# Layer norms whose centre is first taken from the first tiles, in a four-layer hybrid transformer

## The chip, the cores and the metric

One core of a Trainium2 chip runs the whole program. The metric is the device time of one execution in microseconds. PE is TensorE (PEld its weight loads), DVE VectorE, ACT ScalarE, POOL GpSimd, SP SyncE, which issues most DMAs.

## What is computed

```
for i in range(DEPTH):                       # 4 layers: attention, gated delta net, gated linear attention, attention
    mod = (s_lat @ ada_w[i] + ada_b[i]).reshape(bsz, 6, 1, d)      # d = 1024, and modc likewise from s_ctx
    u = modulate(x, mod[:, 0], mod[:, 1])                          # t * (1 + scale) + shift
    y, yc = mixer(u, uc, ...)
    x = layer_norm(DN_ALPHA * x + mod[:, 2] * y, ln_g[i, 0], ln_b[i, 0])
    h = modulate(x, mod[:, 3], mod[:, 4])
    x = layer_norm(DN_ALPHA * x + mod[:, 5] * conv_glu(h, ...), ln_g[i, 1], ln_b[i, 1])
    # the same for the 256 context tokens, in all layers but the last
def layer_norm(t, g, b):
    mu = jnp.mean(tf, -1, keepdims=True)
    var = jnp.mean(jnp.square(tf - mu), -1, keepdims=True)
    return ((tf - mu) * lax.rsqrt(var + NORM_EPS)).astype(t.dtype) * g + b
```

All in float32. There are 256 context tokens and 256 others, 512 columns in all; in the last layer only 256 are carried past the keys and values.

## The kernel before

The residual stream x lies transposed: eight tiles of 128 features, each 128 partitions by 512 tokens. A layer norm's sums therefore run over partitions and tiles, and PE makes them. Every float32 product of weights and activations is three products in fp32r: both operands are split into a rounded high part and a low rest (w_hi, w_lo by POOL, lines 586 and 589; u_hi by ACT, line 697; u_lo by DVE, line 1765). Weights come in units of 1 MB, in two buffers, and are split in four pieces each. The order on each engine is written out by hand, an engine's instructions run in that order, and semaphores count between engines.

A norm (w = 0 after the mixer, w = 1 after the feed-forward part) goes like this. `residual` (DVE, line 1770) adds a finished tile from PSUM to x, two instructions. `mean_sum` (PE, line 1538) sums a tile of x over its features into strips of 32 partitions, four float32 matmuls that show as eight instructions. In w = 0 the last two tiles are made by `tile_unit` (line 1102), one after the other, with mean sums between them; in w = 1 the last down unit finishes tile after tile (line 1704). When all eight tiles are summed, ACT copies the strips to `srow` (line 942), `rows_of` (PE, line 1544) spreads them over 128 partitions, `norm` on DVE subtracts the mean from eight tiles (line 2278), ACT squares each (`norm_stats`, line 950), PE sums the squares (`variance_sums`), ACT takes the root (line 953), DVE the reciprocal (line 2282), PE spreads it, and DVE multiplies (line 2287). Then `make_u` on ACT scales and shifts each tile (line 693) and rounds it, DVE takes the rest with `u_low`, PE starts the next unit's products (`column_unit`, line 1090) tile after tile, and POOL writes the new x (`new_x`, line 598), released by the same u_hi.

While a norm after a mixer runs, PE also makes four of the next layer's conditioning products (`ada_block_unit`, line 1513), whose weights ACT requests. DVE shifts the condition columns for them (`condition_moved`). At the start of the program layer 0's first conditioning products (`ada_unit`, 1504) read eight blocks of 1 MB; their sums are copied (`ada_copy`), turned into columns (`ada_turn`) and made into scale and shift (`modulation`); the first `make_u` follows.

In attention, PE transposes two blocks of probabilities into banks 4 and 5 (line 1171), ACT copies both at once (line 731).

```
def variance_sums(l, w):
    for t in range(KT):
        eng.wait_ge(sq_ready, pe.next(sq_ready))
        mm = strips(l, bank[STAT[w][1]], meanw[:, 0:32], sq[:, t % 4, :], t == 0, t == KT - 1)
        mm.then_inc(var_ready if t == KT - 1 else sq_used, 1)
    eng.wait_ge(dev_ready, pe.next(dev_ready))
    rows_of(l, bank[STAT[w][3]]).then_inc(rstd_ready, 1)
```

## Time and profile before

| | |
|---|---|
| median of 3 runs | 2803.31 us (2802.9, 2803.31, 2812.05) |
| the profiled execution | 2810.65 us, of which the span is 2808.9 |
| PE busy | 2617.1 us (93%) |
| POOL, DVE, ACT busy | 1559.1, 1166.7, 828.2 us |
| granted TensorE clock, mean | 0.966 of full |

A row of a timeline gives start, length, engine, line, operation, what is written and read with shapes, the count of instructions in it, and in brackets the idle time before it and what ended that. A row that merges several instructions gives the time from the first one's start to the last one's end.

### The profile page before, as it was taken

To read this page: it belongs to the slowest core of one execution; us is meant where nothing else is said; L and a number is where in the kernel's file an instruction comes from. 1 tells how busy PE (TensorE), PEld (TensorE's weight loads), DVE (VectorE), ACT (ScalarE), POOL (GpSimd) and SP (SyncE) were. 2 spreads that over 40 slices of the span, in tenths; PEclk is the share of its full clock that TensorE was granted. 3 is DMA by queue.
4 is the path that set the end of the run, shared out by engine and by line. 5 is a ranking of instruction groups with operands and counts; after the bars stand their busy time and mean duration, and the time that the engine had idled before them with its cause. 6 is when DMAs were issued, how large, how long until landed. Compare 5 with 4: busy or idle time off the path is not lost. (4 is left out here: it accounts for less than half of the span.)

```text
span 2808.9 us, 45504 instructions
## 1 busy us (share of the span) xinstructions
PE 2617.1 (93%) x16413; PEld 2105.6 (75%) x16413; DVE 1166.7 (42%) x2177; ACT 828.2 (29%) x1556; POOL 1559.1 (56%) x1601
## 2 busy tenths in 40 slices
PE   6999999999899799999999989898999999787998
PEld 4766677787687699767778768896677787677997
DVE  2364322222469677432222320584322222463555
ACT  2253322211540444142210132351312211353542
POOL 2402666666558222466667656785666665715664
PEclk8999999999999899999999989999999999898998
DMA  6343455423123000255542222002455422201553
GB/s 243 115 132 123 156 172 167 155 91 102 50 76 90 31 2 2 90 165 179 177 132 95 75 63 90 31 1 75 152 178 179 150 90 90 75 31 61 180 177 108
DMA packets 217162, 305.61 MB, mean 109 GB/s; under 512 B 7331, under 2 KB 155550, under 8 KB 217023
## 3 DMA queue, kind: packets, MB, share of 16 engines
q1 hardware_dynamic: 179007, 228.16, 24.6%
q10 hardware_dynamic: 38016, 75.50, 8.3%
q8 instruction: 98, 1.61, 0.2%
q14 instruction: 41, 0.34, 0.0%
HBM read 302.60 MB, written 1.05 MB: 108 GB/s over the span
## 5 line engine op out<-in xcount | busy, mean ns | idle before, releaser
L589 POOL TENSOR_TENSOR w_lo<-w_raw,w_hi 128x512 fp32r<-128x512 f32 x688 | 900.6, 1309 | 102.3 <-POOL w_hi L586 82.2
L586 POOL TENSOR_SCALAR w_hi<-w_raw 128x512 fp32r<-128x512 f32 x688 | 450.7, 655 | 880.5 <-PE bank L1090 597.0
L1090 PE MATMUL bank<-u_lo,w_hi 128*128 128x512 f32 (+1 forms) x2144 | 810.8, 378 | 31.2 <-DVE u_lo L1765 20.2
L1090 PE MATMUL bank<-u_hi,w_lo 128*128 128x512 f32 (+1 forms) x2144 | 793.6, 370 | 0.0
L1090 PE MATMUL bank<-u_hi,w_hi 128*128 128x512 f32 (+1 forms) x2144 | 793.3, 370 | 0.0
L1090 PEld LDWEIGHTS bank<-u_lo,w_hi 128*128 128x128 f32 x2144 | 410.5, 191 | 167.3 <-issue 89.7
L1090 PEld LDWEIGHTS bank<-u_hi,w_hi 128*128 128x128 f32 x2144 | 410.4, 191 | 68.9
L1090 PEld LDWEIGHTS bank<-u_hi,w_lo 128*128 128x128 f32 x2144 | 411.4, 192 | 63.2
L1673 PE MATMUL bank<-gs_lo,w_hi 128*128 128x512 f32 (+1 forms) x576 | 211.4, 367 | 2.2 <-POOL w_lo L589 2.2
L1673 PE MATMUL bank<-gs_hi,w_lo 128*128 128x512 f32 (+1 forms) x576 | 210.8, 366 | 0.0
L1673 PE MATMUL bank<-gs_hi,w_hi 128*128 128x512 f32 (+1 forms) x576 | 210.8, 366 | 0.0
L2360 DVE SCALAR_TENSOR_TENSOR cv<-bank,vec,cv 128x510 f32<-128x510 f32 (+1 forms) x88 | 59.5, 676 | 344.4 <-ACT cv L1010 344.4
L2385 DVE TENSOR_TENSOR gs_lo<-g,gs_hi 128x512 fp32r<-128x512 f32 (+1 forms) x88 | 102.1, 1171 | 239.7 <-ACT gs_hi L1047 239.5
L1010 ACT ACT_TABLE_LOAD x27 | 34.6, 1283 | 431.2 <-PE bank L1090 431.2
L2377 DVE TENSOR_TENSOR g<-cv,bank 128x512 f32 (+3 forms) x88 | 50.8, 617 | 229.1 <-PE bank L1090 218.8
L1047 ACT ACTIVATE gs_hi<-g 128x512 fp32r (+3 forms) x88 | 49.4, 574 | 314.6 <-PE bank L1673 256.2
L1770 DVE SCALAR_TENSOR_TENSOR x<-bank,gat,x 128x256 f32<-128x256 f32 x112 | 48.7, 479 | 192.2 <-PE bank L1090 95.1
L1673 PEld LDWEIGHTS bank<-gs_lo,w_hi 128*128 128x128 f32 x576 | 108.2, 188 | 23.2 <-issue 3.6
L1673 PEld LDWEIGHTS bank<-gs_hi,w_lo 128*128 128x128 f32 x576 | 108.4, 188 | 19.5
L1673 PEld LDWEIGHTS bank<-gs_hi,w_hi 128*128 128x128 f32 x576 | 108.2, 188 | 19.5
L598 POOL TENSOR_SCALAR x<-x,vec 128x512 f32<-128x512 f32 (+1 forms) x56 | 67.5, 1204 | 64.7 <-ACT u_hi L697 64.7
L618 POOL TENSOR_TENSOR bAT<-bD,con 128x512 f32<-128x512 f32 x16 | 20.3, 1273 | 129.5 <-ACT bD L832 129.5
(334 smaller groups left out, 3835.8 us busy)
## 6 DMA issues: line engine op xcount, KB each, us to landing
w_raw<-in_ffn_w_up SPq DMA_DIRECT2D x88, 1024.0 KB, 7.2
ada_w<-in_ada_w ACTq DMA_DIRECT2D x72, 1024.0 KB, 5.2
w_raw<-in_ffn_w_down SPq DMA_DIRECT2D x44, 1024.0 KB, 4.9
ada_w<-in_ada_w SPq DMA_DIRECT2D x16, 1024.0 KB, 5.1
w_raw<-in_gdn_w_in SPq DMA_DIRECT2D x16, 1024.0 KB, 5.7
w_raw<-in_attn_w_qkv SPq DMA_DIRECT2D x12, 1024.0 KB, 5.0
w_raw<-in_gla_w_in SPq DMA_DIRECT2D x12, 1024.0 KB, 5.3
ada<-in_ada_w SPq DMA_DIRECT2D x8, 1024.0 KB, 13.4
```

Source lines behind the costliest of these rows:

```text
L586: eng.tensor_scalar(w_hi[:, q, :], src, 1.0, 0.0, ALU.mult, ALU.add).then_inc(pool.own, pool.step())
L589: eng.tensor_tensor(w_lo[:, q, :], src, w_hi[:, q, :].bitcast(F32), ALU.subtract).then_inc(w_split, 1)
L598: eng.tensor_scalar(x[:, t, T], x[:, t, T], vec[:, LNG(l, w, t):LNG(l, w, t) + 1], vec[:, LNB(l, w, t):LNB(l, w, t) + 1], ALU.mult, ALU.ad ...
L618: eng.tensor_tensor(AT[:], Dm[:], wide(tri[d]), ALU.mult).then_inc(pat_ready, 1)
L1010: eng.activation(cv[:, m, T], bank[m][:, T], ACT.Identity, bias=vec[:, bass.ds(f + CONVB(l), 1)], scale=vec[:, bass.ds(f + CONVW(l, 1), 1) ...
L1047: eng.activation(gs_hi[:, slot, T], gf, ACT.Copy).then_inc(gs_h, 1)
L1090: mm = eng.matmul(bank[banks[m]][:, T], w[:, q, c:c + P], v[:, k, T], start=(k == 0 and n == 0), stop=(k == KT - 1 and n == 2))
L1673: mm = eng.matmul(bank[b][:, T], w[:, q, j * P:(j + 1) * P], v[:, s, T], start=(start and q < 2 and n == 0), stop=(stop and q >= 2 and n = ...
L1770: ins = eng.scalar_tensor_tensor(x[:, t, half(s)], bank[b][:, half(s)], gat[:, l, w, t, s:s + 1], x[:, t, half(s)], ALU.mult, ALU.add)
L2360: eng.scalar_tensor_tensor(v3(cv[:, m, :], 1, 256), v3(bank[m][:], 0, 255), w0, v3(cv[:, m, :], 1, 256), ALU.mult, ALU.add).then_inc(dve.o ...
L2377: eng.tensor_tensor(g[:, bass.ds(i * 2 + m, 1), T].rearrange("p a n -> p (a n)"), cv[:, m, T], bank[2 + m][:, T], ALU.mult).then_inc(g_don ...
L2385: eng.tensor_tensor(gs_lo[:, slot, T], gf, gs_hi[:, slot, T].bitcast(F32), ALU.subtract).then_inc(gs_ready, 1)
```

## The change: a provisional centre, a split start, single copies

Norms. From the first tiles (four of eight in w = 0, two in w = 1; `CENTRE`) a provisional mean is taken and spread over the partitions by one fp32r product per 128 tokens while the last tiles are being multiplied. It is subtracted from each tile as it is finished (`centred`), or ahead of its residual for the last tiles (those from `RAW` on). Squares of the centred tiles are summed in the order `SQUARES`, most of them between the last tiles' products. At the end the true mean's distance d from the centre comes from the same strips; the variance is the mean square less d squared, and each tile is corrected by a second subtraction (`move`), two tiles ahead of the product with the inverse deviation. The conditioning products move: one between the two spreadings, one behind them, two into the first unit of the up projection, behind its tiles 0 and 1.

Start. The conditioning blocks are read in the order 0, 2, 1, 3; after the first four (of eight halves) tiles 0 to 3 are modulated, and the other halves are multiplied ahead of tile 0 and tile 3 of the first projection. The first projection's weights are read in between, the masks behind everything.

Attention. Each transposed block is copied by itself.

```
@@ variables and loads
-STAT = ((4, 5, 6, 4), (0, 1, 2, 7))
+STAT = ((4, 5, 6, 4, 2), (0, 1, 2, 7, 3))
+CENTRE = (4, 2)
+RAW = (6, 4)
+SQUARES = ((0, 1, 6, 2, 3, 4, 5, 7), (4, 0, 5, 1, 6, 2, 7, 3))
             for n in range(ADA_FIRST):
+                if n == ADA_FIRST // 2:
+                    load(column(a["attn_w_qkv"][0], 0))
...
@@ ACT, norm_stats
-                eng.wait_ge(ms_ready, act.next(ms_ready))
-                eng.activation(srow[strips, :], bank[STAT[w][0]][strips, 0:P], ACT.Copy).then_inc(mc_ready, 1)
+                eng.wait_ge(cs_ready, act.next(cs_ready))
+                eng.activation(drow[strips, :], bank[STAT[w][0]][strips, 0:P], ACT.Copy)
+                eng.activation(crow[strips, :], bank[STAT[w][0]][strips, 0:P], ACT.Copy, scale=KT / CENTRE[w]).then_inc(cc_ready, 1)
...
@@ ACT, attention
-                        eng.wait_ge(pt_ready, act.next(pt_ready))
-                        eng.activation(apt[:, j % 3, :, 0:NK], banks[:, 4:6, 0:NK], ACT.Copy).then_inc(pts_ready, 1)
+                        for m in range(2):
+                            eng.wait_ge(pt_ready, act.next(pt_ready))
+                            eng.activation(apt[:, j % 3, m, 0:NK], bank[4 + m][:, 0:NK], ACT.Copy).then_inc(pts_ready, 1)
@@ PE, w = 0
+                    if m == 0 and inside:
+                        eng.wait_ge(cc_ready, pe.next(cc_ready))
+                        centre_rows(l, 0)
+                    elif m == 0:
                         for t in (4, 5):
                             mean_sum(l, 0, t)
+                    elif inside:
+                        mean_sum(l, 0, 6)
+                        for i in range(4):
+                            square_sum(l, 0, i)
                     else:
...
+                        for i in range(4, 7):
+                            square_sum(l, 0, i)
+                        mean_sum(l, 0, 7)
@@ PE, w = 1, behind down tile t
+                    if t == 3:
+                        eng.wait_ge(cc_ready, pe.next(cc_ready))
+                    if t >= 1:
+                        mean_sum(l, 1, t - 1)
+                    if t == 3:
+                        centre_rows(l, 1)
+                    for i in {5: (0,), 6: (1, 2), 7: (3, 4)}.get(t, ()):
+                        square_sum(l, 1, i)
@@ DVE, norm
+                eng.wait_ge(ms_ready, dve.next(ms_ready))
+                eng.tensor_tensor(drow[strips, :], drow[strips, :], bank[STAT[w][0]][strips, 0:P], ALU.add).then_inc(dl_ready, 1)
...
+                eng.tensor_tensor(d2row[strips, :], drow[strips, :], drow[strips, :], ALU.mult).then_inc(dve.own, dve.step())
...
+                    eng.tensor_tensor(srow[strips, :], bank[STAT[w][1]][strips, 0:P], d2row[strips, :], ALU.subtract).then_inc(vr_ready, 1)
...
                 for t in range(KT + 1):
                     if t < KT:
+                        eng.wait_ge(dve.own, moved[t])
                         ins = eng.tensor_tensor(x[:, t, S], x[:, t, S], rstd, ALU.mult)
...
+                        if t + 2 < KT:
+                            move(t + 2)
+                    if t == 1 and behind:
+                        behind()
                     if t >= 1 and not final:
                         u_low(l, t - 1)
@@ PE, start, behind each u tile's wait of the first projection
+            def first_tile(k):
+                if k == 0:
+                    ada_half_block(2)
+                if k == 1:
+                    ada_turn(ADA_ORDER[2])
+                if k == 3:
+                    ada_half_block(3)
+                    ada_turn(ADA_ORDER[3])
+                u_tile(k)
```

What stands on PE behind the last tile of w = 0 in layer 0, before (a row of 32x128 is a strip sum, of x for the mean or of sq for the variance; L1544 spreads rows, L1513 is a conditioning product):

```order
L1513 MATMUL bank<-ada_w,sT 32x512 [waits tile_finished,ada_loaded_0]
L1513 MATMUL bank<-ada_w,sT 32x512 x3
L1538 MATMUL bank<-x,con 32x128 [waits residual_ready]
L1538 MATMUL bank<-x,con 32x128 x3
L1538 MATMUL bank<-x,con 32x128 [waits residual_ready]
L1538 MATMUL bank<-x,con 32x128 x3
L1544 MATMUL bank<-srow,con 128x128 [waits mean_strips_copied]
L1544 MATMUL bank<-srow,con 128x128 x3
L1513 MATMUL bank<-ada_w,sT 32x512 [waits ada_loaded_1]
L1513 MATMUL bank<-ada_w,sT 32x512 x3
L1538 MATMUL bank<-sq,con 32x128 [waits square_ready]
L1538 MATMUL bank<-sq,con 32x128 x3
```

After the change, the same place from the last mean sum on (L1575 strip sums, L1581 spreads rows, L1545 conditioning), three more square sums standing ahead of it:

```order
L1575 MATMUL bank<-x,con 32x128 [waits residual_ready]
L1575 MATMUL bank<-x,con 32x128 x3
L1575 MATMUL bank<-sq,con 32x128 [waits square_ready]
L1575 MATMUL bank<-sq,con 32x128 x3
L1581 MATMUL bank<-drow,con 128x128 [waits mean_from_centre_ready]
L1581 MATMUL bank<-drow,con 128x128 x3
L1545 MATMUL bank<-ada_w,sT 32x512 [waits ada_loaded_0]
L1545 MATMUL bank<-ada_w,sT 32x512 x3
L1581 MATMUL bank<-srow,con 128x128 [waits inverse_deviation_ready]
L1581 MATMUL bank<-srow,con 128x128 x3
L1545 MATMUL bank<-ada_w,sT 32x512 [waits ada_loaded_1]
L1545 MATMUL bank<-ada_w,sT 32x512 x3
```

The mean sum of tile 6 and four square sums have left this place; they now stand in the middle of the last tile's products:

```order
L1575 MATMUL bank<-x,con 32x128 [waits residual_ready]
L1575 MATMUL bank<-x,con 32x128 x3
L1575 MATMUL bank<-sq,con 32x128 [waits square_ready]
L1575 MATMUL bank<-sq,con 32x128 x3
L1575 MATMUL bank<-sq,con 32x128 [waits square_ready]
L1575 MATMUL bank<-sq,con 32x128 x3
L1575 MATMUL bank<-sq,con 32x128 [waits square_ready]
L1575 MATMUL bank<-sq,con 32x128 x3
L1575 MATMUL bank<-sq,con 32x128 [waits square_ready]
L1575 MATMUL bank<-sq,con 32x128 x3
L1132 MATMUL bank<-u_lo,w_hi 128x512
L1132 MATMUL bank<-u_hi,w_lo 128x512
```

On DVE, from the last residual to the first u_lo, before (L1770 residual, L2278 subtraction, L2282 reciprocal, L2287 product with the inverse deviation, L1765 u_lo):

```order
L1770 SCALAR_TENSOR_TENSOR x<-bank,gat,x 128x256 [waits tile_finished]
L1770 SCALAR_TENSOR_TENSOR x<-bank,gat,x 128x256
L2278 TENSOR_TENSOR x<-x,bank 128x512 [waits mean_ready]
L2278 TENSOR_TENSOR x<-x,bank 128x512 x7
L1779 COPY sT_kept<-sT 128x240 [waits ada_multiplied]
L1782 MEMSET sT 128x8x2 [waits dve_step]
L1783 COPY sT<-sT_kept 128x8x30
L2282 RECIPROCAL srow<-srow 128x128 [waits deviation_ready]
L2287 TENSOR_TENSOR x<-x,bank 128x512 [waits inverse_deviation_rows_ready]
L2287 TENSOR_TENSOR x<-x,bank 128x512
L1765 TENSOR_TENSOR u_lo<-u_66,u_hi 128x512 [waits u_hi_ready]
```

After the change (L1868 residual, L2391 and L2393 the distance and its square, L2406 the variance, L2399 correction, L2425 product):

```order
L1868 SCALAR_TENSOR_TENSOR x<-bank,gat,x 128x256 [waits dve_step,tile_finished]
L1868 SCALAR_TENSOR_TENSOR x<-bank,gat,x 128x256
L2391 TENSOR_TENSOR drow<-drow,bank 128x128 [waits mean_strips_ready]
L2393 TENSOR_TENSOR d2row<-drow 128x128 [waits mean_from_centre_ready]
L2406 TENSOR_TENSOR srow<-bank,d2row 128x128 [waits variance_ready,dve_step]
L2411 RECIPROCAL srow<-srow 128x128 [waits deviation_ready]
L2399 TENSOR_TENSOR x<-x,bank 128x512 [waits mean_ready]
L2399 TENSOR_TENSOR x<-x,bank 128x512
L2425 TENSOR_TENSOR x<-x,bank 128x512 [waits dve_step,inverse_deviation_rows_ready]
L2399 TENSOR_TENSOR x<-x,bank 128x512
L2425 TENSOR_TENSOR x<-x,bank 128x512 [waits dve_step]
L2399 TENSOR_TENSOR x<-x,bank 128x512
```

The eight subtractions have left the place behind the last residual, and each product is now followed by a correction two tiles ahead; the first u_lo follows three rows of condition columns later.

## Rows read from the trace of the kernel before

**Rows 1.** Busy time by stretch of the span, core 0, the columns as its head says
```profile
core 0: us, PE busy (x) PEld busy (x) DVE busy (x) ACT busy (x) POOL busy (x), PEclk, DMA share, GB/s
0.00:48.50 48.50, 22.63 (x136) 13.64 (x136) 12.21 (x26) 4.28 (x8) 5.14 (x10) 0.88 0.87 309
299.60:315.90 16.30, 12.66 (x129) 5.50 (x129) 9.33 (x18) 8.10 (x15) 8.30 (x9) 0.81 0.59 195
709.30:725.50 16.20, 8.38 (x104) 4.61 (x104) 8.78 (x15) 8.01 (x15) 8.19 (x9) 0.71 0.00 0
2576.40:2587.40 11.00, 5.85 (x50) 3.81 (x49) 5.54 (x14) 5.08 (x14) 7.99 (x9) 0.80 0.17 49
```

**Rows 2.** Timeline of layer 0's first norm: start us, length, engine, line, operation
```profile
286.95 0.64 PE L1538 MATMUL bank<-x,con 128*32 128x128 f32 x16
...
299.62 0.87 DVE L1770 SCALAR_TENSOR_TENSOR x<-bank,gat,x 128x256 f32<-128x256 f32 x2 [5.41 <-PE bank L1102]
...
302.82 4.87 DVE L2278 TENSOR_TENSOR x<-x,bank 128x512 f32<-128x512 f32 x8 [2.32 <-PE bank L1544]
...
308.90 0.37 ACT L953 ACTIVATE srow<-bank,con 128x128 f32<-128x128 f32 x1 [0.55 <-PE bank L1538]
309.30 0.95 DVE L2282 RECIPROCAL srow<-srow 128x128 f32<-128x128 f32 x1 [1.09 <-ACT srow L953]
...
310.30 2.08 PE L1544 MATMUL bank<-srow,con 128*128 128x128 f32 x8 [1.48 <-DVE srow L2282]
...
312.31 3.64 PE L1513 MATMUL bank<-ada_w,sT 128*32 128x512 f32 x16
312.42 1.28 DVE L2287 TENSOR_TENSOR x<-x,bank 128x512 f32<-128x512 f32 x2 [2.17 <-PE bank L1544]
...
313.22 1.09 ACT L693 ACTIVATE u<-x,aff 128x256 f32<-128x256 f32 x2 [3.96 <-DVE x L2287]
...
314.35 0.63 ACT L697 ACTIVATE u_hi<-u 128x512 fp32r<-128x512 f32 x1
...
315.01 0.69 DVE L1765 TENSOR_TENSOR u_lo<-u,u_hi 128x512 fp32r<-128x512 f32 x1 [1.31 <-ACT u_hi L697]
315.08 1.26 POOL L598 TENSOR_SCALAR x<-x,vec 128x512 f32<-128x512 f32 x1 [7.43 <-ACT u_hi L697]
```

**Rows 3.** Timeline of layer 0's second norm, same columns
```profile
698.21 0.88 DVE L1770 SCALAR_TENSOR_TENSOR x<-bank,gat,x 128x256 f32<-128x256 f32 x2 [0.45 <-PE bank L1704]
...
707.28 0.43 PE L1538 MATMUL bank<-x,con 128*32 128x128 f32 x8
...
709.34 0.88 DVE L1770 SCALAR_TENSOR_TENSOR x<-bank,gat,x 128x256 f32<-128x256 f32 x2 [1.07 <-PE bank L1704]
...
710.76 0.28 ACT L942 ACTIVATE srow<-bank 128x128 f32<-128x128 f32 x1 [24.42 <-PE bank L1538]
...
711.09 1.16 PE L1544 MATMUL bank<-srow,con 128*128 128x128 f32 x8 [0.40 <-ACT srow L942]
...
722.11 1.28 DVE L2287 TENSOR_TENSOR x<-x,bank 128x512 f32<-128x512 f32 x2 [2.17 <-PE bank L1544]
```

**Rows 4.** Timeline of the last layer's first norm
```profile
2585.19 0.75 DVE L2287 TENSOR_TENSOR x<-x,bank 128x256 f32<-128x256 f32 x2 [0.80 <-PE bank L1544]
```

**Rows 5.** DMA rate in 40 slices of the first 70 us, and a timeline row
```profile
GB/s 0 271 285 7 357 358 233 407 405 407 398 387 382 392 386 383 392 386 383 392 385 383 353 349 347 125 1 0 0 0 195 380 25 0 0 0 0 74 368 162
...
48.49 0.77 PE L1090 MATMUL bank<-u_lo,w_hi 128*128 128x512 f32 x1 [3.61 <-DVE u_lo L1765]
```

**Rows 6.** Timeline of POOL and DVE in the first make_u, and u_lo's min/median/max ns
```profile
45.96 1.26 POOL L589 TENSOR_TENSOR w_lo<-w_raw,w_hi 128x512 fp32r<-128x512 f32 x1
...
47.19 0.62 POOL L586 TENSOR_SCALAR w_hi<-w_raw 128x512 fp32r<-128x512 f32 x1
...
47.45 0.90 DVE L1765 TENSOR_TENSOR u_lo<-u,u_hi 128x512 fp32r<-128x512 f32 x1 [2.05 <-ACT u_hi L697]
...
L1765 DVE TENSOR_TENSOR u_lo<-u,u_hi x64: 424/692/1820, 47.5 to 2593.5; 128x512 fp32r<-128x512 f32 x56, 128x256 fp32r<-128x256 f32 x8
```

**Rows 7.** ACT's waits from 131 to 262 us (total, times, longest), and a timeline row
```profile
ACT apt L731 <- PE bank L1171: 38.3, 32, 2.9
...
2485.42 1.02 ACT L731 ACTIVATE apt<-bank 128x1024 f32<-128x1024 f32 x1 [0.72 <-PE bank L1171]
```

More of the change, by code:

```diff
@@ L2270, in upper, with centred @@
                 dve.skip(w_done, 4)
-            def norm(l, w, final=False, behind_mean=None):
+            def centred(l, w, t, ahead=False):
                 S = toks(l)
-                mean = bank[STAT[w][2]][:, S]
-                strips = slice(S.start // P * 32, P)
-                eng.wait_ge(mean_ready, dve.next(mean_ready))
-                for t in range(KT):
-                    eng.tensor_tensor(x[:, t, S], x[:, t, S], mean, ALU.subtract).then_inc(c_ready, 1)
-                if behind_mean:
-                    behind_mean()
-                eng.wait_ge(std_ready, dve.next(std_ready))
-                eng.reciprocal(srow[strips, :], srow[strips, :]).then_inc(dev_ready, 1)
-                rstd = bank[STAT[w][3]][:, S]
+                ins = eng.tensor_tensor(x[:, t, S], x[:, t, S], bank[STAT[w][2]][:, S], ALU.subtract)
+                if ahead:
+                    ins.then_inc(dve.own, dve.step())
+                else:
+                    ins.then_inc(c_ready, 1)
@@ L2334, in _ @@
                         dve.skip(w_done, 4)
+                        centre_seen(l, 0)
+                        for t in (6, 7):
+                            centred(l, 0, t, ahead=True)
+                        ahead = dve.count()
+                        for t in (0, 1):
+                            centred(l, 0, t)
                     for m in range(2):
@@ L2337, in _ @@
                             eng.wait_ge(tile_done, dve.next(tile_done))
+                            eng.wait_ge(dve.own, ahead)
                         residual(l, 0, 2 * n + m, (n % 2) * 2 + m)
+                        if (n, m) == (3, 0):
+                            for t in range(2, RAW[0]):
+                                if t >= CENTRE[0]:
+                                    eng.wait_ge(raw_read, dve.next(raw_read))
+                                centred(l, 0, t)
                 more = l + 1 < LAYERS
-                norm(l, 0, behind_mean=condition_moved if more else None)
+                norm(l, 0, behind=condition_moved if more else None)
                 per = {conv_c: 2, silu_done: 2, w_done: 8, own["dve"]: 2}
```

242 lines of the change are left out of this document (168 added, 74 removed).

## The prediction

> **What bounds the kernel now.** TensorE is busy nearly all the time, so a change can only pay where it waits. I read first the table of stretches, from a sublayer's last tile to the next one's first product, and the start [rows 1]. The reader is to see that such a stretch lasts 16.3, 16.2 and (last layer, half the tokens) 11.0 us, that PE's work in it is small products in half to three quarters of the time, and that the granted clock averages 0.71 to 0.81. There are eight of them, three of each of the first two kinds and two of the third: 3 x 16.3 + 3 x 16.2 + 2 x 11.0, some 120 of 2809 us. The start passes 48.5 us before the first projection.
>
> The timeline of one norm after the mixer [rows 2] gives the chain. Let T be the start of the last residual (299.62). The mean's rows are there at T+3.2, where eight subtractions start; squares follow at their pace until the root at T+9.3; reciprocal, rows at half clock (2.08 us), and the first product with the inverse deviation starts at T+12.8; call that moment R. From R on ACT sets the pace: 1.09 + 0.63 us a tile, measured 1.66 with the overlap; PE starts at R+3.5. The norm after the feed-forward part has the same chain, T = 709.34, R = T+12.8 [rows 3].
>
> **The norm after the mixer, three layers of 512 tokens.** Into PE's busy time come two detours from the tile products. What a detour costs: residuals come 0.88 + 0.45 us apart without a mean sum between the tiles and 0.88 + 1.07 with one [rows 3], some 0.6 more (I count 0.58; a tile is six products there, one each 0.22 to 0.23). Sixteen of its small instructions show as 0.64, eight as 0.43 [rows 2, 3], so a sum costs 0.2 and leaving the tile products 0.38. The four centre products cost at most a sum's 0.2: 0.6 us with the detour. Mean of tile 6 and four square sums: 0.38 + 5 x 0.2 = 1.4. T moves by +2.0. DVE gets eight provisional subtractions (0.61 us from start to start, 4.87 for eight [rows 2]) between the residuals; a tile is 24 products, 5.5 us on PE, so they fit.
>
> Behind T, with row durations: residual 0.88, strips at 1.42 [rows 3], a 128x128 addition I take as 0.2 (bounds: nothing and the 0.37 of ACT's root [rows 2]) gives 1.65. Beside it the square, a pass of ACT like u_hi's 0.63, and its sum 0.43 with 0.2 of latency give the variance at 2.15, the subtraction 2.4, root 0.37, reciprocal 0.95: 3.8. On PE the mean's rows (1.16 at full clock [rows 3]) end at 3.1, the conditioning product that stands between at 4.15 (1.8 at half clock, two in 3.64 [rows 2]; 1.07 at full), the deviation's rows at 5.4. DVE corrects tiles 0 and 1 meanwhile. R = old T + 2.0 + 5.4 = T+7.4 where T+12.8 was: **5.4 us** earlier.
>
> Not all of it lasts. Each of six tiles now has a correcting subtraction between its product and its u_lo: 0.61 + 0.61 + 0.69 = 1.9 us on DVE against ACT's 1.66. Counted through (moving the condition columns too, 0.65 us ahead of the first u_lo), the last u_lo comes at R+15.9, before it was R+14.8: 1.1 back. The two conditioning products that filled the wait now stand behind tiles 0 and 1 of the up projection, 1.07 each at full clock and 1.8 at half; PE's slack per tile is 1.9 - 1.37, so that most hides; I take 0.5 back, between 0 and 2.7 (6.8 us at half clock would cost 3.4 on PE, of which 0.7 lies under POOL's rounding of the next piece). Net 3.8 a norm, **11.4 us** for three. Their second weights are requested behind tile 0's u_hi, beside the next up weights: 0 to 2 us late, in the same bound.
>
> **The norm after the feed-forward part, three layers.** One more detour (0.58), the centre rows 0.2, three square sums 0.6, and 0.1 where the square of tile 5 comes late: T+1.45. DVE now does subtraction, residual, subtraction per tile, 2.2 us, against PE's 2.0 to 2.3: even. After T: two raw tiles are still to be centred (to 2.15), three squares in ACT's order end at 3.4, their sums, then mean rows at 3.1 to 4.3, the last square's sum 4.65, difference, root, correction of tile 0, reciprocal at 6.4, rows at 7.7, or 8.6 at half clock. Half clock is nearer: this stretch has 0.71 [rows 1], and the rows of this step took 2.08 in rows 2. R saves 12.8 - 1.45 - 8.65 = 2.7; the slower loop returns 0.4 (no moving of columns). Net 2.3, **6.9 us** for three.
>
> **The last layer** has 256 tokens: R-T is 8.7, from the stretch's start to 2585.19 [rows 1, 4]. By halved durations (0.34 from one product to the next: two end 0.75 after the start, one lasts 0.41) the first norm gets 1.3 + 4.1, gain 3.3, loop back 0.5: **2.8**. The final norm gains 2.2 and does six subtractions more in its last loop, 6 x 0.34: **0.2**.
>
> **Squared mean on DVE.** It reads SBUF twice while POOL rounds pieces. In the start such an operation, u_lo, took 0.90 where 0.69 is usual, and ended 0.54 after POOL's instruction [rows 6]. The new one can wait nothing or a piece's w_lo, 1.26; most of its wait is covered by the square's sum; 0.2 x 7: **-1.4 us**. The Trainium skill, page "SBUF — State Buffer", section "Who interferes with whom", says that a VectorE instruction with two SBUF inputs and a GpSimd instruction that reads SBUF exclude each other for a whole instruction; by that rule the term's upper end is right.
>
> **The start.** Before, all eight conditioning blocks are read first: the first product is at 48.49 [rows 5]. DMA moves 380 to 390 GB/s there, 2.7 us for a block of 1 MB [rows 5]. Now masks move behind, and four blocks suffice for tiles 0 to 3. I get the fourth block at 27, modulation at 31 to 32, u_lo(0) at 35; but PE then reads blocks five and six before tile 0 (landed at 35), and seven and eight before tile 3. At half clock (6 x 0.43 a tile, twice the above, 1.8 a pair of blocks) tile 3 is reached at 50 and tile 7 ends near 61, at full clock near 55. Before it ended near 62 (eight tiles from 48.49 by ACT's 1.66). Gain 1 to 7; **3 us**, nearer to half clock, since PE is mostly idle there. The mask's cast (1.16) stands before the last u_lo, its cost is in the 61.
>
> **Attention.** ACT's copy of both transposes (1.02 [rows 7]) becomes two, 0.6 each by u_hi's 0.63; the first starts half a transpose set earlier and the last ends 0.4 earlier, if ACT is free; it waited 38.3 us for transposes in 32 pairs [rows 7]. Between 16 x 0.2 lost (layer 3, if ACT binds) and 0.4 in half of 48 pairs won: -3 to +9, I take **2 us**, below the middle, as PE is the bound of most pairs.
>
> **Sum**: 11.4 + 6.9 + 2.8 + 0.2 - 1.4 + 3 + 2 = 24.9. The profiled execution took 2810.65, so it would take 2786. It stands 7.3 above the median of the runs, 2803.31; against that I forecast **2778 us**. 0.5% is 14 us, about what a measurement of this kernel can tell.
>
> **Rivals.**
> A, the clock stays up. Today rows of 1.2 us take 2.1, the conditioning products 1.8. If the shorter wait keeps full clock, 0.9 more for each rows step and 0.8 to 1 in the first unit: about 2 us x 7, gain 39, **2763 us**. For it: the gap shrinks by a third. Against: today it falls although sums run in between.
> B, the first up or projection unit gives it back. With half clock over its first 7 us PE needs 2.57 a tile against 1.9 supplied, and late conditioning weights add up to 2. Then 1.5 a mixer norm, 0.5 a feed-forward norm, 1.5 in the last layer, 1 at the start: gain 8.5, **2795 us**. For it: the end of the unit, not its start, passes the gain on. Against: six columns' u_lo already came slower than PE's 1.37.
> C, slower: u_lo is locked out by POOL. Until now u_lo and POOL's new x (L598) are released by the same u_hi, and DVE goes 70 ns ahead: 0.69 for u_lo, 1.26 for POOL [rows 2]. Now DVE is in a product or correction at that moment and POOL starts first. If u_lo then loses 0.9 (the longest seen, 1.82 [rows 6], loses 1.13), 56 times, it is 50 us: **2828 us**. The whole gain is gone from 25 / 56 = 0.45 us each. Against: POOL's 1.26 includes its wait behind u_lo, 0.6, so alone it should last some 0.7 and be over when DVE comes to u_lo, about 0.7 after u_hi. If 1.26 were POOL's true length, u_lo would wait 0.5 more a tile: 28 us, **2806**. That a lock lasts for the whole instruction is what the page named above says of it.
> That the change does not do what it says can be at the start: tiles 0 to 3 wait for the later blocks anyway. That is in B.
>
> **Chances.** Forecast (2768 to 2788) 0.50; A 0.15; B 0.26; C 0.09. Faster: the forecast, A and the best edge of B, 0.67. Same: the rest of B, 0.24. Slower: C, 0.09. The forecast's own range is 2768 to 2788; down to 2755 takes in A with attention's upper bound, up to 2805 takes in B with a start of nothing and attention lost.
>
> **What would show it.** In a mixer norm, R at T+5 to 6 from the last residual, the tile 7 later by 2; in a feed-forward norm T+8 to 9. DVE's period 1.9 in the first unit and its u_lo at 0.69; if it is over 1.1, C. The table of stretches should show some 11 and 13 us instead of 16.3, and the unit behind 0.5 to 1 more. First product of a projection near 36, but the second unit of projections only about 3 us earlier. Wrong would be: square sums that wait in the tile products for over 0.5 us, a first unit longer by over 3 us, or a start that gains nothing.

## The result and the profile after

The changed kernel takes 2774.60 us (median of 6 runs, 2771.59 to 2777.97), the kernel before 2803.11 (6 runs, 2799.18 to 2812.05): ratio 0.9899, 95% interval 0.9882 to 0.9917, 28.5 us less. The forecast was 2778. The profiled execution took 2774.4, its span is 2772.6; before they were 2810.65 and 2808.9, so the two traces lie 36.3 us apart, 8 more than the medians.

The stretches of [rows 1], in the changed kernel, same columns (busy time by stretch):

```profile
core 0: us, PE busy (x) PEld busy (x) DVE busy (x) ACT busy (x) POOL busy (x), PEclk, DMA share, GB/s
0.00:37.10 37.10, 16.23 (x103) 9.24 (x103) 10.43 (x24) 8.06 (x13) 7.11 (x12) 0.94 0.90 321
295.20:305.00 9.80, 5.95 (x74) 3.26 (x73) 8.51 (x17) 4.37 (x8) 8.41 (x10) 1.00 0.45 134
699.00:710.20 11.20, 4.69 (x74) 3.14 (x73) 8.65 (x16) 4.79 (x10) 8.22 (x9) 0.91 0.00 0
2541.00:2548.20 7.20, 2.77 (x29) 2.04 (x29) 5.60 (x13) 2.45 (x6) 6.55 (x8) 0.99 0.00 0
```

The stretches of 16.3, 16.2 and 11.0 us have become 9.8, 11.2 and 7.2 us, and the granted clock stays at 1.00, 0.91 and 0.99 where it was 0.81, 0.71 and 0.80. So far the stretches did better than forecast. As in the prediction, T is the start of a norm's last residual and R the start of its first product with the inverse deviation. The chain in layer 0's first norm, which answers to [rows 2] (timeline; T is 295.24):

```profile
295.24 0.88 DVE L1868 SCALAR_TENSOR_TENSOR x<-bank,gat,x 128x256 f32<-128x256 f32 x2 [4.48 <-PE bank L1132]
...
296.99 0.59 DVE L2393 TENSOR_TENSOR d2row<-drow 128x128 f32<-128x128 f32 x1
...
297.19 1.16 PE L1581 MATMUL bank<-drow,con 128*128 128x128 f32 x8
...
297.94 0.40 ACT L978 ACTIVATE srow<-srow,con 128x128 f32<-128x128 f32 x1 [1.16 <-DVE srow L2406]
...
298.38 0.95 DVE L2411 RECIPROCAL srow<-srow 128x128 f32<-128x128 f32 x1 [0.47 <-ACT srow L978]
...
299.38 1.16 PE L1581 MATMUL bank<-srow,con 128*128 128x128 f32 x8
...
300.58 0.69 DVE L2425 TENSOR_TENSOR x<-x,bank 128x512 f32<-128x512 f32 x1
```

R is at T+5.34, forecast T+5.4; the deviation's rows take 1.16 us, not 2.08. What comes behind R is where the forecast was too kind:

```profile
302.98 0.47 DVE L1877 COPY sT_kept<-sT 128x240 f32<-128x240 f32 x1
...
303.50 0.72 DVE L1881 COPY sT<-sT_kept 128x240 f32<-128x240 f32 x1
...
304.14 0.67 DVE L1863 TENSOR_TENSOR u_lo<-u,u_hi 128x512 fp32r<-128x512 f32 x1
...
304.96 0.47 PE L1118 MATMUL bank<-u_lo,w_hi 128*128 128x512 f32 x1 [3.42 <-DVE u_lo L1863]
...
307.38 1.77 PE L1545 MATMUL bank<-ada_w,sT 128*32 128x512 f32 x8
307.73 0.93 DVE L1863 TENSOR_TENSOR u_lo<-u,u_hi 128x512 fp32r<-128x512 f32 x1
...
310.66 1.06 PE L1545 MATMUL bank<-ada_w,sT 128*32 128x512 f32 x8
```

The first product now starts at R+4.38 (before R+3.47), since the condition columns are moved ahead of the first u_lo. The conditioning products take 1.77 us at half clock and 1.06 at full; PE works without a gap up to the second unit at 321.08. The half clock has not gone. It has moved out of the stretch into the first unit's opening: from 305.0 to 309.0 the granted clock is 0.57. In the kernel before it was 0.50 from 312.0 to 316.0, ahead of the unit, and 0.91 in the unit's first 4 us.

By norm, from both traces (before to after; "tile stage" is from the first product of the last 48 ahead of T up to T, "unit" from R to the first product of the second unit):

```
                     tile stage      R-T                      unit                        in all
mixer, layers 0-2    12.1 to 14.0    12.8/13.0/13.0 to 5.34   17.8/17.9/17.8 to 20.5/21.5/20.4   -2.8/-2.1/-3.0
feed-fwd, 0-2        14.1 to 16.0    12.8 to 7.7/8.6/8.5      23.9/27.4/17.6 to 25.0/28.5/18.6   -2.1/-1.2/-1.5
mixer, layer 3       10.2 to 11.7     8.7 to 4.9              11.4 to 12.6                       -1.2
final                 8.5 to 10.1     8.6 to 6.0              12.6 to 14.3 (to the end)          +0.6
```

That is 13.3 us in all for the eight norms, where 19.9 were forecast (11.4 + 6.9 + 2.8 + 0.2 - 1.4). What made the total right anyway was in no step of the forecast. Busy time of the down projection's 432 products in the kernel before (layer 0, then layer 3), then in the one after:

```profile
594.30:695.00 100.70, 100.69 (x432) 81.12 (x432) 1.00 0.28 94
2726.70:2777.60 50.90, 50.13 (x432) 49.64 (x432) 1.00 0.49 166
```
```profile
585.00:682.90 97.90, 97.88 (x432) 81.00 (x432) 1.00 0.29 97
2688.70:2741.10 52.40, 52.03 (x432) 51.86 (x432) 1.00 0.48 160
```

The same 432 products at the same full clock take 2.8 us less in each of layers 0 to 2 (8.5 us in all) and 1.5 more in layer 3. The change has no hunk in that loop. But its new buffer one_r takes 64 bytes ahead of g, gs_hi and gs_lo (g is the gated activation that the down projection reads, gs_hi and gs_lo are its two halves). By the program's sizes, counted from its first buffer, w_hi, w_lo, u_hi and u_lo lie at multiples of 128 bytes in both kernels; gs_hi and gs_lo lay 64 past one before and lie on one now.

### The profile page after: what moved, and what is told of

Same layout as the page of the kernel before. It is cut to its first block and busy times, and to the rows that moved or that the text cites. A ratio compares the mean times of both kernels' runs of the same rounds, so it can differ in the third digit from the quotient of the medians.

```text
span 2772.6 us, 45769 instructions
## 1 busy us (share of the span) xinstructions
PE 2592.8 (94%) x16441; PEld 2100.9 (76%) x16441; DVE 1211.5 (44%) x2278; ACT 838.6 (30%) x1614; POOL 1544.2 (56%) x1601
## 3 DMA queue, kind: packets, MB, share of 16 engines
HBM read 302.60 MB, written 1.05 MB: 110 GB/s over the span
## 5 line engine op out<-in xcount | busy, mean ns | idle before, releaser
L1118 PE MATMUL bank<-u_lo,w_hi 128*128 128x512 f32 (+1 forms) x2144 | 811.1, 378 | 39.2 <-DVE u_lo L1863 26.9
L2539 DVE TENSOR_TENSOR g<-cv,bank 128x512 f32 (+3 forms) x88 | 50.8, 618 | 228.2 <-PE bank L1118 217.9
L1868 DVE SCALAR_TENSOR_TENSOR x<-bank,gat,x 128x256 f32<-128x256 f32 x112 | 48.7, 480 | 161.1 <-PE bank L1118 93.4
L1038 ACT ACTIVATE cv<-bank,vec 128x512 f32<-128x512 f32 (+1 forms) x88 | 58.8, 718 | 105.8 <-PE bank L1118 105.5
## 6 DMA issues: line engine op xcount, KB each, us to landing
ada<-in_ada_w SPq DMA_DIRECT2D x8, 1024.0 KB, 13.6
```

The costliest lines, as they stand in the source:

```text
L1038: eng.activation(cv[:, m, T], bank[m][:, T], ACT.Identity, bias=vec[:, bass.ds(f + CONVB(l), 1)], scale=vec[:, bass.ds(f + CONVW(l, 1), 1) ...
L1118: mm = eng.matmul(bank[banks[m]][:, T], w[:, q, c:c + P], v[:, k, T], start=(k == 0 and n == 0), stop=(k == KT - 1 and n == 2))
L1868: ins = eng.scalar_tensor_tensor(x[:, t, half(s)], bank[b][:, half(s)], gat[:, l, w, t, s:s + 1], x[:, t, half(s)], ALU.mult, ALU.add)
L2539: eng.tensor_tensor(g[:, bass.ds(i * 2 + m, 1), T].rearrange("p a n -> p (a n)"), cv[:, m, T], bank[2 + m][:, T], ALU.mult).then_inc(g_don ...
```

## The experiments

Each was timed together with the kernel before on the same chip; its ratio to that is what is compared.

**1. The 64 bytes alone.**

```diff
         warm = sb("warm", [P, 1])
+        pad = sb("pad", [P, 16])
```

> The kernel before with 64 unused bytes behind the buffer `warm`, so that every buffer of the layer stages (the gated g, its halves gs_hi and gs_lo, q, k, v) lies 64 bytes higher, as the new buffer one_r puts it in the changed kernel; not an instruction differs. Theory 'layout': the place of gs_hi and gs_lo sets the rate of the down projection; its 432 products then take 97.8 us instead of 100.7 in each of layers 0 to 2 and 52.4 instead of 50.9 in layer 3, and the kernel is some 7 us faster (2796). Rival 'instructions': the down projection gained through the changed work between its products; then the loop stays at 100.7 and the time at 2803.

Measured 0.9973 (0.9961 to 0.9984), 7.6 us faster. The loop in this run, layers 0 and 3:

```profile
593.90:691.80 97.90, 97.90 (x432) 81.00 (x432) 1.00 0.29 97
2713.10:2766.00 52.90, 52.23 (x431) 51.90 (x432) 1.00 0.48 159
```

**2. The change without them.** The buffer is laid into unused bytes.

```diff
-        one_r = sb("one_r", [P, TT], F32R)
+        one_r = sb("one_r", [P, TT], F32R, at=top[0] - 32)
```

> The changed kernel with one_r laid into the unused bytes behind `warm`, so that the buffers of the layer stages lie where they lay before the change; not an instruction differs. Theory 'layout': the down projection goes back to 100.7 us (layer 3 to 50.9) and the kernel takes 7 us more than the changed one, 2782. Rival 'instructions': loop 97.8, time 2775.

Measured 0.9939 (0.9924 to 0.9954), median 2786.88: 11 us slower than the change by the ratios. The loop in layers 0 and 3:

```profile
586.90:687.60 100.70, 100.69 (x432) 81.12 (x432) 1.00 0.28 94
2705.40:2756.80 51.40, 50.23 (x432) 49.90 (x432) 1.00 0.48 164
```

Theory "layout" holds in both directions, and some 7 to 11 of the 28.5 us are a side effect. The loops themselves account for 7 of them (three times 2.8, less 1 to 2 in layer 3).

**3 and 4. Attention alone, start alone.** The edits are the diff's hunks of these two parts on the kernel before.

> The kernel before with only the copy of the transposed probabilities split in two. By the prediction's term: 2 us faster (between 3 slower and 9 faster), 2801; the attention stages themselves then show it. Rival: ACT has no time to spare in these pairs, and the second instruction per pair costs 0.2 each, 48 of them, so 2806 or more, or in layer 3 alone 3 us. Down projection as before, 100.7.

Measured 0.9984 (0.9973 to 0.9995): 4.5 us faster, 1.4 to 7.5. This run's own trace can't place it: from the second projection unit to T, layer 3's mixer takes 155.3 us, and the four traces with unchanged attention and unchanged norms have it anywhere from 155.4 to 158.2. Beside the changed norms it shows: up to the tile stage the same stretch takes 144.9 us with the old copy (experiment 5, one trace) and 140.5 to 142.1 in the eight traces with the new one. So layer 3 gained some 3 us there, and the prediction's loss in layer 3, if ACT binds, did not come.

> The kernel before with only the changed start (four conditioning blocks ahead of tiles 0 to 3, masks later, the rest between the tiles of the first unit). By the prediction: 3 us faster (1 to 7); the changed kernel's trace has the end of the first unit at 57.5 instead of 62.5, so 5 us and 2798 if all of that reaches the end; first product at 37, end of the first unit 57.5. Rival: the masks and weights that now come later, or the conditioning work in the unit, cost it again within the attention of layer 0, then 2801 to 2803.

Measured 0.9993 (0.9980 to 1.0005): 2 us faster, between 1.4 slower and 5.6 faster, so the gain is not clear of noise. Its trace has the first unit's end at 58.1 instead of 62.5. Other runs with the same start suggest why the median says less. The changed kernel, then the run of experiment 6, both from 37 us on (busy time by stretch):

```profile
37.00:49.00 12.00, 9.74 (x56) 6.73 (x53) 3.85 (x9) 2.95 (x6) 2.97 (x3) 0.91 0.98 344
```
```profile
37.00:49.00 12.00, 11.19 (x50) 7.96 (x49) 2.58 (x4) 1.78 (x4) 2.68 (x3) 0.70 0.99 346
```

At clock 0.91 the fourth u_lo ends at 48.5 and the unit at 57.5; at 0.70 at 50.8 and 60.4. Of the nine traces with this start, five end the unit at 57.3 to 58.1 and four at 60.3 to 60.5. So at the end of the unit the start is worth 5 us in some executions and 2 in others, by the granted clock while PE works on the late conditioning blocks. How many of the unprofiled executions were of either kind is not known. The rival, that layer 0's attention gives some of it back, stays open too: in the eight traces with the same start and attention, the stretch from the second projection unit to the tile stage lasts anywhere from 221.0 to 223.9 us.

**5. The norms alone**, start, attention and place of every buffer as before.

> The kernel before with the changed norms alone: start and attention are as before, and one_r lies in unused bytes, so that no buffer moves. By the prediction's sum (11.4 + 6.9 + 2.8 + 0.2 - 1.4) 19.9 us faster, 2781. By the segments of the changed kernel's trace, with the tile stages 1.9 us longer and the first units given back, only 13 us: 2787 to 2789. If it is 19.9, the segments were read wrong (the clock differed between the two traces).

Measured 0.9971 (0.9961 to 0.9981), 8.1 us faster (5.3 to 10.9). That is not the forecast's 19.9, and it is less than the 13.3 of the table by norm too. In layers 0 to 2 R comes at T+5.34 after the mixer and the tile stages are 14.0 and 16.0 us, as in the changed kernel. But in this trace the last tile stage of layer 3's mixer takes 14.05 us and not 11.7: its products come 0.213 us apart, half clock, and not 0.120. The same eight segments as in the table add up to 328.3 us in this run's own trace, to 325.1 in the changed kernel's and to 338.2 in the kernel before. So this execution gained 10 us in the norms, within the interval. Of the nine traces with the changed norms, four have this half clock in layer 3, 2.4 us each time. The norms are worth 8 to 13 us, 40 to 67% of the forecast, and part of the spread is that clock.

The four parts measured alone add up to 22 us (norms 8.1, start 2, attention 4.5, the 64 bytes 7.6), the whole change to 28.5. Each part is uncertain by some 3 us either way and the whole by 5, so this doesn't show that the parts help each other.

**6. Without the corrections in the loop.**

```diff
-                    eng.tensor_tensor(x[:, t, S], x[:, t, S], mean, ALU.subtract).then_inc(dve.own, dve.step())
+                    if t < 2:
+                        eng.tensor_tensor(x[:, t, S], x[:, t, S], mean, ALU.subtract).then_inc(dve.own, dve.step())
```

> The changed kernel without the correcting subtractions of tiles 2 to 7 (the mean of these tiles stays off by the small rest that the provisional mean leaves). By the prediction's term DVE's 1.9 us a tile is what gives 1.1 us a norm back: the last u_lo comes at R+14.8 instead of R+16 to 16.8, and each of the six norms of 512 tokens gains 1.1, the last two 0.5 and 2: 8 us, 2767. Rival: in the norm after the mixer PE is the one that is behind (its products and the two moved conditioning products run without a gap from tile 2 on), so there the unit after starts no earlier; only the norm after the feed-forward part gains: 3 x 1.1 + 2, 2769 to 2770.

Measured 0.9868 (0.9843 to 0.9893), median 2767.0, 8.7 us less than the change by the ratios. The last u_lo comes at R+14.8 after the feed-forward part and the second unit 1.1 earlier behind R, as both theories had it. After the mixer the last u_lo is 1.8 earlier (R+15.0), and PE starts 0.8 earlier, since no correction stands ahead of the first u_lo. But the unit, measured on PE from its first product to its 48th's end, takes 15.1, 15.2 and (once) 13.6 us where the change has 15.2, 16.2 and 15.1: hardly shorter although DVE's pace is. The second unit starts 0.9, 1.8 and 2.3 earlier. So the time met the first figure (its interval would allow the second too), and neither mechanism is the whole: the rival's "no earlier" is wrong, as PE's start had not been thought of.

**7 and 8. The moved conditioning products.** First one product in place of four (`parts` is how many are made).

```diff
-                        ada_block_unit(k - 1)
+                        ada_block_unit(k - 1, parts=1)
```

> The changed kernel with one small product in place of the four of each of the two conditioning units that stand in the first unit of the up projection (the modulation of the next layers is then not the right one). By the prediction's term they cost 0.5 us a norm: the second unit starts 0.5 earlier, 1.5 in all, 2773. Rival: the moved products stand on the path whole but for what the last u_lo sets, 1.3 us of their 2.8 a norm, 4 us in all, 2771; they are the larger part of what the norm after the mixer gives back.

Measured 0.9899 (0.9876 to 0.9921), the same as the change. The edit took no time away, which its timeline shows at once:

```profile
308.84 1.86 PE L1545 MATMUL bank<-ada_w,sT 128*32 128x512 f32 x2
...
312.19 1.05 PE L1545 MATMUL bank<-ada_w,sT 128*32 128x512 f32 x2
```

Two instructions take as long as eight did (1.77 and 1.06), so the four lie side by side. The Trainium skill says so of products that fill only 32 rows or columns (page "TensorE: Matmul & The Clock Gate", section "Part 3: Packing small matmuls — row/col tiling"): they run at the same time in different parts of the array. By that the trace agrees, and the run says nothing on the price. So the columns were cut instead, 512 to 32:

```diff
-                        ada_block_unit(k - 1)
+                        ada_block_unit(k - 1, cols=32)
```

> The changed kernel with the two conditioning units inside the first up unit cut from 512 to 32 columns each (the modulation of the later layers is then not the right one), since one product in place of four took as long as the four. By the prediction's term (0.5 a norm): 1.5 us, 2773. If PE's own queue of work sets the end of that unit, it ends earlier by what was taken away up to the last u_lo's 1.3 us, the second unit at T+24.5 instead of 25.8: 4 us, 2770.

Measured 0.9884 (0.9869 to 0.9899), 4.2 us less than the change by the ratios, a difference that the two intervals leave open. The second unit starts at T+25.3, 25.2, 25.1 instead of 25.8, 26.9, 25.8: 3.0 us for three norms, and 2.3 to 3.3 us against the three other traces with these norms and the full products. The moved products cost some 1.0 a norm, not 0.5.

**9. Which place matters.** The kernel before with the pad ahead of everything:

```diff
+        pad = sb("pad", [P, 16])
         con = sb("con", [P, K_N])
```

> The kernel before with the 64 unused bytes ahead of every buffer, so that the weights (w_hi, w_lo) and u_hi, u_lo, which lay at multiples of 128 bytes, now lie 64 bytes past one, and gs_hi, gs_lo the other way round. Theory M, the place of the moving operand decides: the down projection takes 97.8 us in layers 0 to 2 as with the pad behind `warm`, but the up loop's products (0.227 us apart) go to 0.233, some 1056 a layer, 7 us more, so a feed-forward part takes 379 - 3 + 7 = 383 us instead of 379, and with the projections (some 2200 products) the kernel is 20 to 30 us slower, 2820 to 2830. Theory R, the moving operand must lie as the stationary one does: nothing changes at all, down 100.7, time 2800.

Measured 0.9997 (0.9983 to 1.0012). The down loop is at 100.70 with gs on a multiple of 128 bytes and the weights 64 past one (counted from the first buffer of the kernel before), and the up loop's median spacing stays 0.227 us. It is the two operands' places against each other that count, theory R; theory M falls. Every other buffer ahead of g moved along with the weights here, so that the partner is the weights, and not another of these, is the likely reading and was not tested by itself. The loop in layers 0 and 3 of this run:

```profile
591.90:692.60 100.70, 100.68 (x432) 81.12 (x432) 1.00 0.29 94
2715.50:2766.30 50.80, 49.61 (x431) 49.23 (x432) 1.00 0.49 166
```

**10. The tails reordered.**

```diff
-SQUARES = ((0, 1, 6, 2, 3, 4, 5, 7), (4, 0, 5, 1, 6, 2, 7, 3))
+SQUARES = ((0, 1, 6, 2, 3, 4, 5, 7), (4, 0, 5, 1, 6, 7, 2, 3))
...
-                for i in (5, 6):
+                for i in (5, 6, 7):
                     square_sum(l, 1, i)
                 mean_rows(l, 1)
-                square_sum(l, 1, 7)
...
                 variance()
-                if w == 0:
-                    inverse()
+                inverse()
                 eng.wait_ge(mean_ready, dve.next(mean_ready))
                 move(0)
-                if w == 1:
-                    inverse()
                 move(1)
...
-                    if t == 1 and behind:
-                        behind()
                     if t >= 1 and not final:
                         u_low(l, t - 1)
+                    if t == 1 and behind:
+                        behind()
```

> The changed kernel with three moves. After the feed-forward part: PE sums the last square before it broadcasts the mean, ACT squares tile 7 before tiles 2 and 3, and DVE takes the reciprocal before the first correction; R should come at T+7.2 instead of T+7.7 to 8.6 (1.4 less, three times, and 1 in the last layer). After the mixer: DVE makes the first u_lo before it moves the condition columns, so PE starts 0.95 earlier after R, 3.4 instead of 4.4. If PE is behind in that unit, as the rival of the run without corrections has it, all 0.95 reach the end: 3 x 1.2 + 1 + 3 x 0.95 = 7.5 us, 2767. If DVE's pace bounds the unit (the prediction's term), the second part gives nothing: 2770.

Measured 0.9873 (0.9851 to 0.9894), median 2770.55, 7.3 us less than the change by the ratios and 4 by the medians; the time alone can't tell 2767 from 2770, the traces can. After the feed-forward part of layer 0 (timeline; T is 698.09):

```profile
700.87 0.43 PE L1575 MATMUL bank<-sq,con 128*32 128x128 f32 x8 [0.17 <-ACT sq L974]
701.23 1.16 PE L1581 MATMUL bank<-drow,con 128*128 128x128 f32 x8
...
702.19 0.95 DVE L2410 RECIPROCAL srow<-srow 128x128 f32<-128x128 f32 x1 [0.47 <-ACT srow L978]
...
704.40 0.69 DVE L2421 TENSOR_TENSOR x<-x,bank 128x512 f32<-128x512 f32 x1
```

R is at T+6.31 in all three, where T+7.2 was expected, and at T+5.05 instead of 6.02 in the last. After the mixer:

```profile
303.03 0.69 DVE L1862 TENSOR_TENSOR u_lo<-u,u_hi 128x512 fp32r<-128x512 f32 x1
...
303.64 0.27 DVE L1876 COPY sT_kept<-sT 128x240 f32<-128x240 f32 x1
303.87 0.47 PE L1118 MATMUL bank<-u_lo,w_hi 128*128 128x512 f32 x1 [2.47 <-DVE u_lo L1862]
```

PE starts at R+3.43 again and the second unit at T+25.0 in all three, 0.8, 1.9 and 0.8 earlier, although the last u_lo comes no sooner (R+16.7). The unit takes PE 15.0 to 15.1 us again. In layers 0 and 1 that is PE's own length, as in experiment 6 with a last u_lo at R+15.0, half clock at its opening included. In layer 2 no product runs at half clock, experiment 6 took 13.6 there, and here the six products behind the last u_lo end the unit at R+18.4. In layers 0 and 1 it ends at R+18.5 and 18.6. So with the earlier start PE and the last u_lo are even, and PE's start was what had put the end later than the last u_lo does. After the feed-forward part the second unit starts 2.2 us earlier in layers 1 and 2; in layer 0 it doesn't (T+33.0, the change 32.7; experiment 11, with the same code there, 31.3), which stays open.

**11. Four places of gs.** The reordered kernel with

```diff
+        GS_PLACE = ((32, 32), (96, 96), (0, 64), (64, 64))
```

> The reordered kernel, with another place of gs_hi and gs_lo in each layer, counted from a multiple of 128 bytes, where the weights lie: layer 0 both at 32, layer 1 both at 96, layer 2 gs_hi at 0 and gs_lo at 64, layer 3 both at 64. If any difference from the weights' place costs, layers 0 and 1 take 100.6 us for 432 products and layer 2 between 97.8 and 100.6 (two of three products read gs_hi: 98.7, if each pays for itself; 100.6, if a change between the operands pays). If only the 64 bytes matter, 97.8 in layers 0 and 1. In layer 3, 64 should give 51 to 52 us instead of 52.4 to 52.9. Whole kernel: 2770.6 of the reordered one plus 3 to 8 us, less 1 in layer 3.

Measured 0.9896 (0.9881 to 0.9911), 6.4 us more than the reordered kernel by the ratios. The loop in layers 0 to 3 (both at 32; both at 96; gs_hi at 0 and gs_lo at 64; both at 64):

```profile
585.90:686.60 100.70, 100.68 (x432) 80.88 (x432) 1.00 0.29 94
1474.70:1575.40 100.70, 100.70 (x432) 80.99 (x432) 1.00 0.28 94
2251.10:2351.20 100.10, 100.08 (x432) 81.01 (x432) 1.00 0.28 95
2693.60:2745.00 51.40, 51.08 (x432) 50.91 (x432) 1.00 0.48 164
```

Any of the three differences from the weights' place costs the same 2.8 us, and one of two operands misplaced costs nearly all of it (2.3). In layer 3, with 256 columns, the misplaced ones are the faster, but by less and less evenly: from first to last product 50.8 to 52.0 us in the eight traces with gs_hi and gs_lo 64 bytes off, 52.3 to 52.9 in the six with them at the weights' place.

**12. Using it.** The reordered kernel, with u_hi, u_lo, gs_hi and gs_lo of the last feed-forward part 64 bytes further (and every use of them there):

```diff
+        u3_hi = sb("u3_hi", [P, KT, TOK], F32R, at=U0 + 64)
+        u3_lo = sb("u3_lo", [P, KT, TOK], F32R, at=U0 + KT * TOK * 4 + 64)
...
+        gs3_hi = sb("gs3_hi", [P, 4, TOK], F32R, at=AR0 + FT * K4 + 64)
+        gs3_lo = sb("gs3_lo", [P, 4, TOK], F32R, at=AR0 + (FT + 4) * K4 + 64)
```

> The reordered kernel; in the last layer, where a product has 256 columns, the moving operands of the feed-forward part (u_hi, u_lo of the up loop, gs_hi, gs_lo of the down loop) lie 64 bytes further, so 64 past a multiple of 128 while the weights lie on one. In the runs so far a 256-column down product came every 0.113 to 0.118 us there and every 0.120 at the weights' own place, the other way round than with 512 columns. Theory 'place': the some 990 up products come at 0.113 to 0.118 instead of 0.120 too, 2 to 7 us, and the 432 down products gain 1: 3 to 8 us against the reordered kernel (2770.6), 2763 to 2768. Rival: it is a matter of what else runs beside the down loop, and the up products stay at 0.120: 2770.

Measured 0.9855 (0.9836 to 0.9875), median 2762.47 (2760.59 to 2765.74): the fastest of all, 12 us under the change and 39 under the kernel before by the medians. Against the reordered kernel it is 8 us less by the medians and 5 by the ratios, a difference that the two intervals leave open; the theory rests on the spacing of the products in this one trace. Up products in 40 us of the last layer, reordered kernel, then this one:

```profile
2600.00:2640.00 40.00, 40.00 (x336) 40.00 (x335) 1.00 0.57 184
```
```profile
2600.00:2640.00 40.00, 40.00 (x342) 40.00 (x341) 1.00 0.59 190
```

The mean spacing over the loop falls from 0.120 to 0.118, with some 1000 products 2 us; with the down loop's 1.0 (52.3 to 51.4 us) that is 3 us, and no trace places the rest.

## Why the prediction was right, and where it was not

The total was right: 28.5 us measured, 24.9 forecast. That is luck in part. Two errors cancel: the norms gave 8 to 13 us and not 19.9, and a side effect that nobody planned gave 7 to 11.

- **T later.** Mixer +2.0 forecast, +1.9 measured; feed-forward +1.45, measured +1.85; last layer about +1.5 in both norms, against the 1.3 counted into the first. No square sum waited in the tile products. Right. The half clock in layer 3's tile stage, 2.4 us more in four traces of nine, was not foreseen.
- **R after T.** After the mixer T+5.4 was forecast and 5.34 measured. After the feed-forward part T+8.65 at half clock was forecast, measured 7.7 once (with the clock up) and 8.5 to 8.6 twice. Right.
- **The loop behind R.** Forecast 1.1 from DVE's 1.9 a tile and 0.5 for the conditioning products. The last u_lo did slip (from R+14.8 to R+16.8 after the mixer and R+15.9 after the feed-forward part), but the step failed after the mixer: it treated DVE's pace and PE's extra work as two small terms of one chain. PE was the later of the two: six products behind the last u_lo would end at R+18.4 (experiment 10), and they end at R+19.5 to 20.6, where the kernel before had 16.5 to 16.7. So some 1.9 us are the last u_lo's own slip, against 1.1 in the forecast, and 1.1 to 2.2 more are PE's. Its first product came 0.9 later, since moving the condition columns (which I had counted into the last u_lo) stands ahead of the first u_lo; that and the conditioning products, 1.0 a norm by experiment 8, end the unit 2.7 to 3.6 us later behind R. Forecast 1.6. This, three times, is 4 us of the 6.6 that are missing, and the last layer another 2.4. After the feed-forward part the loop gave back 0.9 to 1.1 us, with the last u_lo 0.9 to 1.1 later, where 0.4 was forecast: 2 us in three norms.
- **The last layer.** Forecast 3.0 for both, by the traces 0.6. In the first norm R comes 2.4 us earlier in all (forecast 3.3) and the unit gives back 1.2 (forecast 0.5). The final norm loses 0.6: R comes 1.1 earlier (forecast 2.2), and what follows it, with six corrections, takes 1.7 longer.
- **Squared mean.** It takes 0.59 us after the mixers, 0.75 after the feed-forward parts and 0.79 in layer 3's first norm, against 0.29 in the final norm, where no POOL instruction runs beside it; so it waits 0.3 to 0.5 for POOL. It costs nothing in the feed-forward norms, where the last square's sum ends later. By the rows it costs 3 x 0.3 + 0.5 = 1.4 us, as forecast. The trace agrees with the Trainium skill's rule (page "SBUF — State Buffer", section "Who interferes with whom") in that it waits for POOL, but the term's upper end, a w_lo of 1.26, was not seen.
- **The start.** 3 us forecast, 1 to 7; 2 us by experiment 4, not clear of noise, with 5 at the unit's end in the changed kernel's own trace. In the range as far as it can be told, and the reason given, half clock on the conditioning blocks, goes with 2 or 5 at the unit's end.
- **Attention.** 2 us forecast, 4.5 measured (1.4 to 7.5), in the range.
- **Rival A** came half true: in the mixer norms' stretch the clock stays at 1.00 instead of 0.81. It brought nothing beyond the 5.4, which had counted full clock already, for the half clock came in the unit behind. (By its own sum, gain 39, its figure is 2764 and not 2763.)
- **Rival B** was the mechanism of what went missing: the unit gives back 2.7 to 3.6 us of the 7.5 by which R comes nearer to T, and half clock at its opening came (0.57 from 305.0 to 309.0). Its price of 1.5 a mixer norm was what would be left, and 2.1 to 3.0 were.
- **Rival C** fell. u_lo lasts 0.69 us in the median and 0.75 in the mean of layer 0's first unit; POOL's new x takes 0.77 to 0.79 us when it starts first, and 1.27 when it starts behind u_lo:

```profile
303.29 0.79 POOL L615 TENSOR_SCALAR x<-x,vec 128x512 f32<-128x512 f32 x1
...
315.00 0.69 DVE L1863 TENSOR_TENSOR u_lo<-u,u_hi 128x512 fp32r<-128x512 f32 x1 [0.68 <-ACT u_hi L718]
...
315.07 1.27 POOL L615 TENSOR_SCALAR x<-x,vec 128x512 f32<-128x512 f32 x1 [0.78 <-ACT u_hi L718]
```

  Where DVE comes second while POOL still runs, u_lo takes 0.93 (307.73 above) to 1.03 us, 0.24 to 0.34 more and not 0.9. The argument against C (alone POOL lasts some 0.7) was the right one. The Trainium skill (page "SBUF — State Buffer", section "Who interferes with whom") calls the shared port pair an exclusive lock whose holder is decided by issue order. The trace agrees where the starts lie over 0.3 us apart: the first keeps its own length of 0.77, and the second waits for what is left of it. Of starts within 0.1 us DVE kept its 0.69 to 0.71 each time, also where POOL is shown 0.03 to 0.09 us ahead.
- **Missed altogether:** that a new buffer of 16 bytes, which takes 64, can shift the operands of an untouched loop. The diff showed it in one line; I read that line as storage.

## What to carry to other kernels

A new buffer is a change to every buffer behind it. When a loop that no hunk touches changes its rate at full clock, compare addresses first, and test with an unused pad of the same size: one run. And when a wait in front of a pipeline is shortened, ask for the first item's chain (what stands ahead of the first u_lo, when PE's queue starts) before the pace of the rest; here 0.95 us ahead of the first u_lo counted nearly in full, and the pace of the rest became the limit only when they were gone.

## What the runs showed of the hardware

- A stream of 128x512 fp32r products runs at 0.227 us each where the moving operand lies at the same place within 128 bytes as the stationary one, and at 0.233 on average where it lies 32, 64 or 96 bytes off (97.8 against 100.65 us for 432). Shifting both together changes nothing. The weights alone were never moved, so that they are the partner is not shown by itself.
- With 256 columns it is the other way, and weaker: 432 down products take 52.3 to 52.9 us at the same place (six traces) and 50.8 to 52.0 at 64 bytes off (eight traces), 0.121 to 0.123 against 0.118 to 0.121 each; the up products come 0.118 apart in the one trace with them 64 bytes off and 0.120 to 0.121 in the others. Why is not shown; 32 and 96 bytes were not tried with 256 columns.
- Four products of 512 columns into 32 output rows each take as long as one, 1.06 us at full clock and 1.8 at half (1.05 and 1.86 for one).
- The stretch from 295.2 to 305.0 was granted 1.00 throughout, and the dense products right behind it ran at half clock all the same: the granted clock was 0.57 from 305.0 to 309.0, the conditioning unit at 307.38 took 1.77 us, the one at 310.66 took 1.06.
- Executions of the same code differ by where half clock falls. In layer 3's last mixer tiles the products come 0.120 us apart in five of nine traces and 0.213 in four; in the first unit the granted clock from 37 to 49 us is 0.91 in one trace and 0.70 in another. It is worth 2.4 and 3 us.
